# Four modulation dot products on TensorE instead of VectorE, and VectorE two k chunks ahead in the first loop

## The reference

```python
mod = jax.nn.silu(c) @ w_ada[l] + b_ada[l]
shift, scale, gate = jnp.split(mod[:, None, :], 3, axis=-1)
h = rms_norm(x, g_norm[l]) * (1.0 + scale) + shift
proj = h @ w_in[l]
```

## Time and profile before

| | us |
|---|---|
| median of 3 runs | 1423.1 |
| lowest and highest | 1422.59, 1423.24 |
| the profiled execution | 1423.26 |
| its span, first to last instruction | 1421.4 |
| TensorE busy | 1406.4 (99%) |
| VectorE busy | 830.7 (58%) |
| ScalarE busy | 512.3 (36%) |

### The profile page before, as it was taken

One profiled execution on the slowest core, in us unless ns is written; L12 is line 12 of the kernel. 1 busy time (PEld: TensorE's weight loads), 2 busy tenths in 40 slices (PEclk: granted clock), 3 DMA queues, 4 the chain that ended last, 5 costly groups with the idle time before them and its releaser, 6 DMA issues.

```text
span 1421.4 us, 17231 instructions
## 1 busy us (share of the span) xinstructions
PE 1406.4 (99%) x6709; PEld 1176.8 (83%) x6709; DVE 830.7 (58%) x1362; ACT 512.3 (36%) x925; POOL 378.0 (27%) x206
## 2 busy tenths in 40 slices
PE   8999999999999999999999999999999999999998
PEld 6788888888888888888888888888888887888886
DVE  7887557456466745545474554547498426343586
ACT  7745233531323353132235313223553336111122
POOL 0122111222211122221112222111228874222551
PEclk9999999999999999999999999999999999999999
DMA  8411111143211115210111421111141306333543
GB/s 303 153 60 62 33 31 30 31 162 100 66 53 46 45 39 163 75 45 31 31 30 31 149 74 45 30 30 31 30 152 43 130 5 222 105 117 103 173 135 104
DMA packets 51818, 117.19 MB, mean 82 GB/s; under 512 B 20753, under 2 KB 20881, under 8 KB 51734
## 3 DMA queue, kind: packets, MB, share of 16 engines
q1 hardware_dynamic: 47642, 103.23, 22.7%
q10 hardware_dynamic: 2976, 8.80, 1.9%
q0 software_dynamic: 1120, 4.06, 1.0%
HBM read 100.64 MB, written 15.43 MB: 82 GB/s over the span
## 4 chain that ended last, share of the span: by engine, by line
PE 93%; DVE 2%; POOL 1%; DMA 1%; ACT 1%; issue 1%; SPq 0%; DVEq 0%; POOLq 0%; ACTq 0%
PE banks L532 27%; PE banks L534 27%; PE banks L533 27%; PE banks L833 2%; PE banks L823 2%; PE banks L784 2%; PE banks L790 2%; PE banks L842 1%; DVE s_crow L425 1%; POOL wlo L1597 1%; PE banks L770 1%; PE banks L782 1%; DMA raw_lo<-in_x 1%; PE banks L811 1%; PE banks L800 1%
## 5 line engine op out<-in xcount | busy, mean ns | idle before, releaser
L672 POOL TENSOR_TENSOR wlo<-wraw,whi 128x1024 fp32r<-128x1024 f32 x77 | 198.6, 2579 | 858.5 <-ACT whi L920 841.8
L532 PE MATMUL banks<-h_hi,whi 128*128 128x512 f32 x1000 | 399.8, 400 | 1.8 <-POOL wlo L1597 1.4
L534 PE MATMUL banks<-h_hi,wlo 128*128 128x512 f32 x1000 | 390.6, 391 | 0.0
L533 PE MATMUL banks<-h_lo,whi 128*128 128x512 f32 x1000 | 389.5, 390 | 0.0
L534 PEld LDWEIGHTS banks<-h_hi,wlo 128*128 128x128 f32 x1000 | 187.7, 188 | 40.1
L532 PEld LDWEIGHTS banks<-h_hi,whi 128*128 128x128 f32 x1000 | 188.0, 188 | 39.5 <-issue 3.4
L533 PEld LDWEIGHTS banks<-h_lo,whi 128*128 128x128 f32 x1000 | 188.1, 188 | 36.7
L920 ACT ACTIVATE whi<-wraw 128x1024 fp32r<-128x1024 f32 x75 | 79.1, 1055 | 82.3 <-PE banks L534 72.1
L534 PE MATMUL banks<-whi,h_lo 128*128 128x512 f32 x240 | 93.4, 389 | 0.0
L532 PE MATMUL banks<-whi,h_hi 128*128 128x512 f32 x240 | 93.4, 389 | 0.0
L533 PE MATMUL banks<-wlo,h_hi 128*128 128x512 f32 x240 | 93.4, 389 | 0.0
(11 more groups left out here) (379 smaller groups left out, 2604.6 us busy)
## 6 DMA issues: line engine op xcount, KB each, us to landing
wraw<-in_w_all SPq DMA_DIRECT2D x92, 512.0 KB, 3.7
s_wada<-in_w_ada_cols SPq DMA_DIRECT2D x16, 512.0 KB, 7.4
raw_lo<-in_x SPq DMA_DIRECT2D x8, 512.0 KB, 9.2
mlstm_branch<-xc SPq DMA_DIRECT2D x8, 512.0 KB, 4.3
qm<-group_weights SPq DMA_DIRECT2D x8, 512.0 KB, 5.8
part<-in_w_ada_gate SPq DMA_DIRECT2D x16, 256.0 KB, 3.5
sig_c<-in_w_all SPq DMA_DIRECT2D x8, 512.0 KB, 4.0
um_lo_raw<-mlstm_branch SPq DMA_DIRECT2D x8, 512.0 KB, 5.2
```

The lines of the kernel that those rows point to most:

```text
L532: t_.matmul(out, w_hi, x_hi, start=first, stop=False)
L533: t_.matmul(out, w_hi, x_lo, start=False, stop=False)
L534: return t_.matmul(out, w_lo, x_hi, start=False, stop=last)
L672: nc.gpsimd.tensor_tensor(wlo[:, hi, :], wraw[:, q % 2, :], whi[:, hi, :].bitcast(F32), ALU.subtract).then_inc(w_split, 1)
```

## The change

Parts 0 to 3 (`scale` and `shift` of k = 0 and 1) go to TensorE: eight fp32 matmuls a part, with the 128x128 blocks of `w_ada` as weights, in their natural order, and a single column of silu(c) moving, into one column of PSUM bank 1 or 3 (`turned_part`). On the host only the layout of these four parts changes; each is still one load of 512 KB. VectorE adds the bias out of PSUM, two small additions (`gain`).

```diff
+BY_PE = (0, 1, 2, 3)
...
+    def vector_parts(n):
+        return sum(e not in BY_PE for e in range(n))
+
+    def turned_part(n):
+        return ps[:, (1, 3)[n // 2], n % 2:n % 2 + 1]
...
             if j >= NADA:
-                sp.wait_ge(ada_used, j - NADA + 1)
+                if j - NADA in BY_PE:
+                    sp.wait_ge(ada_turned, BY_PE.index(j - NADA) + 1)
+                else:
+                    sp.wait_ge(ada_used, vector_parts(j - NADA + 1))
             sp.dma_start(wada[:, j % NADA, :], a["w_ada_cols"][j]).then_inc(ada_in[j % NADA], 16)
...
+        def gain(k):
+
+            if 2 * k in BY_PE:
+                dve.wait_ge(ada_turned, BY_PE.index(2 * k + 1) + 1)
+                step(v.tensor_tensor(ms[:, 1, k:k + 1], turned_part(2 * k + 1), bc[:, k:k + 1], ALU.add))
+                step(v.tensor_tensor(ms[:, 2, k:k + 1], turned_part(2 * k), bc[:, KT + k:KT + k + 1], ALU.add))
+            else:
+                dve.wait_ge(ada_used, vector_parts(2 * k + 2))
             v.scalar_tensor_tensor(ms[:, 0, k:k + 1], ms[:, 2, k:k + 1], 1.0, gn[:, k:k + 1], ALU.add, ALU.mult).then_inc(ms_ready, 1)
...
-        modulation(0)
+        modulated(4)
+        gain(0)
+        modulated(5)
+        modulated(6)
+        gain(1)
+        gain(2)
+        modulated(7)
+        gain(3)
         for k in range(KT):
-            if k + 1 < KT:
-                modulation(k + 1)
+            if 1 < k < KT - 2:
+                modulated(2 * k + 4)
+                modulated(2 * k + 5)
+                gain(k + 2)
             dve.wait_ge(h_full, k + 1)
...
+        def modulation(n):
+
+            pe.wait_ge(ada_in[n], 16)
+            for e in range(KT):
+                mm = t_.matmul(turned_part(n), wada[:, n, e * P:(e + 1) * P], cc[:, 1, e:e + 1], start=(e == 0), stop=(e == KT - 1))
+            mm.then_inc(ada_turned, 1)
+
         for t in range(NCH):
             if t == NCH // 2:
                 pe.wait_ge(c_silu, 5)
-                for late in range(NCH // 2, NCH):
-                    pe.wait_ge(tile_in[late], 16)
-                    keep_busy(4, 0)
+                modulation(0)
+                modulation(1)
...
             if k == 0:
-                for t in range(5, NCH):
-                    pe.wait_ge(x_kept, 2 * t + 2)
-                    keep_busy(4, 0)
+                pe.wait_ge(x_kept, 2 * NCH - 2)
+                modulation(2)
+                modulation(3)
+                pe.wait_ge(x_kept, 2 * NCH)
+                keep_busy(4, 0)
                 pe.wait_ge(ms_ready, 1)
                 keep_busy(4, 0)
```

More of the change, by code:

```diff
@@ L277, in setup @@
     ada_in = [sem(f"ada_in{j}") for j in range(NADA)]
+    ada_turned = sem("ada_turned")
     ada_used, gw_split, consts, setup_s = sem("ada_used"), sem("gw_split"), T["consts"], sem("pool_setup")
@@ L416, in normalise, with modulated @@
                 v.tensor_scalar(x_raw[:, t, :], x_raw[:, t, :], xs[:, 5, t:t + 1], None, ALU.mult).then_inc(x_norm, 1)
[L418 to L428, removed]
+        def modulated(n):
+            k, j = n // 2, 2 - n % 2
+            dve.wait_ge(ada_in[n % NADA], 16 * (n // NADA + 1))
+            if vector_parts(n):
+                dve.wait_ge(ada_used, vector_parts(n))
+            v.tensor_tensor_reduce(crow[:, 2, :], wada[:, n % NADA, :], crow[:, 1, :], 1.0,
+                                   bc[:, (j - 1) * KT + k:(j - 1) * KT + k + 1], ALU.mult, ALU.add, ms[:, j, k:k + 1])\
+                .then_inc(ada_used, 1)
+        def gain(k):
[5 more added lines that the diff above has]
+                dve.wait_ge(ada_used, vector_parts(2 * k + 2))
             v.scalar_tensor_tensor(ms[:, 0, k:k + 1], ms[:, 2, k:k + 1], 1.0, gn[:, k:k + 1], ALU.add, ALU.mult).then_inc(ms_ready, 1)
@@ L2190 @@
         "c_row": x["c"],
-        "w_ada_cols": np.stack([x["w_ada"][0, :, j * D + k * P:j * D + (k + 1) * P].T for k in range(KT) for j in (1, 0)]),
+        "w_ada_cols": np.stack([tiles(w) if n in BY_PE else w.T for n, w in
+                                enumerate(x["w_ada"][0, :, j * D + k * P:j * D + (k + 1) * P] for k in range(KT) for j in (1, 0))]),
         "w_ada_gate": x["w_ada"][0, :, 2 * D:], "b_cols": np.ascontiguousarray(x["b_ada"][0, :2 * D].reshape(2 * KT, P).T), "b_gate": np.ascontiguousarray(x["b_ada"][:, 2 * D:]),
```

## The result

| | before | changed |
|---|---|---|
| median, us (runs) | 1423.14 (6) | 1428.03 (6) |
| lowest and highest | 1422.59, 1423.37 | 1426.84, 1430.31 |
| profiled execution, its span | 1423.26, 1421.4 | 1427.3, 1425.4 |

The changed kernel takes 1.0036 of the time before, with a 95% interval of 1.0026 to 1.0047: slower by 4.9 us, more than the 0.2% that the prediction took as the bound of no change. The forecast was 1426.5, the range up to 1430.8. Its runs also lie further apart, 3.5 us against 0.8. Each run has its mean granted clock on record: 0.996 in five of the six and 0.994 in the slowest (1430.31), against 0.999 in the profiled execution of the kernel before.

A forecast was written before the change was run, and what follows sets the result against it. The prediction priced the change by the first matmul on line 532, after a chain over ScalarE, then VectorE: +5.35 us at the start of k=1, -1.95 in the loop, together +3.4, so 1423.1 becomes 1426.5 us; range 1424.0 to 1430.8.

The forecast's parts named there:

- step 1: TensorE, ahead of tile 4: parts 0 and 1 at 0.11 us a load end at 24.55, transposes start 1.48 us later.
- Rival A: New matmuls' weight loads cheap, 0.06 us each: +1.1 us, 1424.2; chance 0.2 together with the case of no effect.
- dear half of B: New matmuls' weight loads at 0.19 us each, nothing overlapping: k=1 starts at 43.1, +7.2 us, 1430.3.
- rival B: Dear loads (+7.2 us, 1430.3) or TensorE's clock falling as fillers go and single-column matmuls hardly stream (+7); chance 0.27.
- step 2: TensorE after tile 6 is kept: parts 2 and 3 end at 32.30, first product with `h_hi` 4 us later, at 33.2.
- 10 x 0.23: TensorE's ten products with `h_hi` of k=0, taken at 0.23 us each, ending at 35.5.
- step 3: Part 7's load, its slot freed by part 2 on TensorE: issued at 30.75, landing 4.3 us later at 35.05.
- step 4: VectorE does part 7 and a gain before the first `h_lo`; TensorE, ready at 35.5, waits 2.2 us until 37.75.
- not late: Loads of part 8 and a weight chunk, queued on SP behind part 2: VectorE comes to part 8 only at 39.
- step 5: TensorE's loop: k=1 starts at 39.25, then 25.5 us without waits to line 532 at 64.75.
- -1.95: Loop from k=1 to line 532: 25.5 us instead of 27.45 with four dot products off VectorE.
- four cases: Chances: the forecast 0.5, cheap loads with no effect 0.2, dear loads or slow clock 0.27, loop's gain alone 0.03.

The follow-up runs named there:

- e1_wide: Changed kernel with the 32 new matmuls moving the same column 128 times (broadcast) instead of once: 1426.09 us, ratio 1.0021 to the kernel before.
- e2_seven_later: Changed kernel with VectorE's dot product of part 7 and the gain of k=3 moved behind the first `h_lo`: 1428.35 us, ratio 1.0043 to the kernel before.
- e6_cost_only: Kernel before, all dot products on VectorE, with 32 unused 128-column fp32 matmuls on TensorE in place of the 24 fillers: 1424.44 us, ratio 1.0010.
- e10_split_spread: Kernel before with only parts 0 and 3 on TensorE, 128 broadcast columns, part 5 ahead of the first `h_lo`, later parts respaced: 1420.91 us, ratio 0.9986.
- e9_split_narrow: Kernel before with only parts 0 and 3 on TensorE, a single column moving, VectorE's parts reordered: 1421.81 us, ratio 0.9992.
- e7_free_parts: Changed kernel with its new matmuls left out and 24 filling transposes in their place, result incomplete: 1425.33 us, ratio 1.0015 to the kernel before.
- e3_wide_seven_later: Changed kernel with 128 broadcast columns moving and part 7 with the gain of k=3 behind the first `h_lo`: 1425.68 us, ratio 1.0020 to the kernel before.

## Why the prediction was right, and where not

The steps, in us, against the two kernels (e1_wide's trace runs 0.4 us late from ahead of the edit, the changed kernel's 0.1):

| | predicted | changed | e1_wide |
|---|---|---|---|
| tile 4's transposes start | 24.55 | 24.64 | 25.01 |
| parts 2 and 3 start | 28.78 | 30.30 | 29.18 |
| part 7: issued, us to landing | 30.75, 4.3 | 32.3, 3.4 | 31.3, 3.6 |
| first product with `h_hi` | 33.2 | 34.72 | 33.64 |
| first product with `h_lo` | 37.75 | 38.64 | 37.55 |
| k=1 starts | 39.25 | 40.07 | 39.05 |
| the three matmuls | 64.75 | 65.48 | 64.47 |

**Loads (step 1).** Right: 0.11 us taken, 3.65/32 = 0.114 measured, for one column and for 128, at the full clock. Rival A (0.06) and the dear half of B (0.19) fall. (Rival A's end of part 1 at 22.6 is a slip: two parts at its 0.93 us end at 22.9, still before 23.07.) The Trainium skill ("TensorE: Matmul & The Clock Gate", section "LDWEIGHTS (loading the stationary operand)") gives the number of columns divided by 1.2 ns, so 107 ns for 128 columns; the trace agrees within 7 ns.

**Delay of tile 4 (step 1).** Right in its start, 1.57 us against 1.48. Wrong in what followed: the transposes take 5.36 us, not 3.71. The step assumed the full clock. This is the half of rival B that I gave 0.27. Its mechanism is shown by e1_wide. Its size was smaller than the +7 worked out: the transposes took 1.65 us more where up to 3.3 were allowed, since the clock came back at 28.5, and parts 2 and 3 took nothing more. For the clock at the very start that rival goes by the pace of the transposes alone: the granted clock's row reads 1.00 there too (10.0 to 15.2 us), with transposes 0.22 us apart. The transposes of e2_seven_later, 32 in 6.56 us where the row reads 0.50, bear its reading out.

**Products of k=0 (step 2).** "10 x 0.23" fails: from the fourth on they start 0.43 apart, at half clock. **Part 7's load (step 3)** was issued 1.55 us late, behind the slow transposes, and was mis-sized, 3.4 for 4.3 us, which gave 0.9 of it back. That the sum came so near owes something to luck: the two errors have opposite signs.

**The wait of 2.2 us (step 4).** It is not there in the changed kernel, since TensorE is late itself, by 0.2 us more than `h_lo`: part 7's load and the slow products end nearly together, and taking part 7 away alone gives nothing (e2_seven_later). With the clock held the wait is 1.34 us, and moving part 7 pays only 0.4 because the loads of parts 8 and 9 are late next. That part 8's load is "not late" was right for the order that the prediction spoke of, and part 9 was left out. VectorE's wait of 2.77 us for part 3 was not named either; it ends before the load does and costs nothing beside it.

**The loop (step 5).** Right: 25.41 us predicted as 25.5, without a wait. But in this kernel it is not a gain of the relief, as e6_cost_only shows: a late TensorE gets 1.79 of it anyway. (In e10_split_spread, where TensorE is not late, the relief does earn it.) I added -1.95 as if the change had earned it; the sum was right, its reading wrong.

**The sum.** +3.4 predicted, +3.1 with the clock held, +4.0 in the profile of the changed kernel and +4.9 in the medians. The forecast is thus the right account of e1_wide and short by the clock for the changed kernel. The last 0.9 us, profile to median, stays open: the profiled execution is among the three faster ones of six, and to three digits its mean clock, 0.996, is that of the runs at 1428.75 and 1428.76 too. Only the slowest, at 0.994, shows more time at the low clock. The chances given have a slip as well: faster 0.02 belongs to none of the four cases.

## What to carry to other kernels

Moving work off the engine that bounds a loop paid here only where it fitted into time in which the other engine truly stood idle: one dot product of 1.8 us fitted into 2.04 us and two did not. Before counting a loop's gain, ask whether a late start alone would give it. Look for the load whose slot comes free last and put its user behind the first result that another engine wants; and where work takes the place of fillers, read what the clock does, since it may have to do their work too.

## What the runs showed of the hardware

The clock was the surprise. Two stretches of 3.6 us of fp32 matmuls with one column were followed by 3.3 and 3.2 us at 0.50 granted clock; the same loads with 128 broadcast columns were as quick (3.65 us for 32) and kept it at 1.00, worth 1.8 to 1.9 us. Two such stretches of half the length (e9_split_narrow) kept it at 1.00 in the profile. A wait of 2.78 us (e7_free_parts) was followed by a fall as well, one of 1.34 (e1_wide) was not. These are cases, not a rule: none of the runs varies the number of columns or the length by steps. The Trainium skill (the same page, "Part 4: PE-mode transpose") holds that transposes don't count as busy time for the clock in the same way; here taking out 24 filling transposes and nothing else was followed by 0.65 granted clock and +2.7 us, so the runs do not bear it out. A 512 KB load landed in 3.4 us when issued to an idle queue (part 7 in the changed kernel) and in 7.2 us beside others (part 9 in e3_wide_seven_later).
